# Row sums for the norms: a moving operand of one column where 128 equal ones stood

## The reference, cut to what matters

```python
def layer_norm(x, g, b):            # twice in each of the 4 layers
    mu = jnp.mean(x32, axis=-1, keepdims=True)
    var = jnp.mean(jnp.square(x32 - mu), axis=-1, keepdims=True)
    y = (x32 - mu) * lax.rsqrt(var + LN_EPS) * g + b

def rms_norm_2(x, w):               # three times in the fifth block
    y = x32 * lax.rsqrt(jnp.mean(x32 * x32, axis=-1, keepdims=True) + RMS_EPS) * w
```

## Time and profile before

| | us |
|---|---|
| median of 3 runs | 3677.93 (3677.74 to 3681.67) |
| the profiled execution's own time | 3677.74 |
| its span in the trace | 3675.9 |
| PE busy | 3564.8 (97%) |
| PE weight loads busy | 2998.0 (82%) |
| DVE busy | 1831.4 (50%) |
| ACT, POOL busy | 941.4 (26%), 824.6 (22%) |
| mean granted clock of TensorE | 0.989 |

### The profile page before, as it was taken

How to read it: one execution, slowest core, us unless ns; L and a number is a source line. 1 busy time by engine, 2 the same in 40 slices (tenths; PEclk the granted TensorE clock), 3 DMA queues, 4 the chain that set the end, 5 groups by cost and what they waited for, 6 DMA issues and landing times.

```text
span 3675.9 us, 44420 instructions
## 1 busy us (share of the span) xinstructions
PE 3564.8 (97%) x18618; PEld 2998.0 (82%) x18618; DVE 1831.4 (50%) x2281; ACT 941.4 (26%) x1662; POOL 824.6 (22%) x374
## 2 busy tenths in 40 slices
PE   8989999999999999999999998999999999999998
PEld 6778888898888888688888877888888887788887
DVE  5555334646563346663336555553464445653434
ACT  2552001312230013540103255210141215120102
POOL 2113222311032223122223211322221111222221
PEclk9999999999999999999999999999999999999999
DMA  5312222221122223122222321222212222222222
GB/s 201 104 58 92 101 95 91 93 69 58 64 81 95 101 92 102 62 75 92 103 93 81 109 81 58 95 92 100 84 69 92 81 92 86 98 92 93 103 92 69
DMA packets 57279, 329.58 MB, mean 90 GB/s; under 512 B 5579, under 2 KB 12235, under 8 KB 20348
## 3 DMA queue, kind: packets, MB, share of 16 engines
q1 hardware_dynamic: 44604, 303.79, 23.1%
q10 hardware_dynamic: 12480, 22.96, 1.8%
HBM read 323.96 MB, written 8.80 MB: 91 GB/s over the span
## 4 chain that ended last, share of the span: by engine, by line
PE 87%; DVE 7%; ACT 3%; issue 1%; DMA 1%; POOL 0%; ACTq 0%; DVEq 0%
PE proj L472 23%; PE proj L474 23%; PE proj L473 23%; PE proj L571 2%; PE proj L573 2%; PE proj L572 2%; DVE s L1740 2%; PE proj L505 2%; PE proj L507 1%; PE proj L506 1%; PE mix L738 1%; PE mix L644 1%; PE mix L549 1%; DVE wlo L1634 1%; PE mix L670 1%; DVE h L1774 1%
## 5 line engine op out<-in xcount | busy, mean ns | idle before, releaser
L451 POOL TENSOR_SCALAR whi<-raw 128x2048 fp32r<-128x2048 f32 x286 | 724.3, 2533 | 2575.8 <-DMA raw<-in_stream 2575.8
L472 PE MATMUL proj<-gh,whi 128*128 128x512 f32 x1968 | 785.7, 399 | 14.4 <-DVE wlo L1640 10.5
L474 PE MATMUL proj<-gh,wlo 128*128 128x512 f32 x1968 | 770.9, 392 | 0.0
L473 PE MATMUL proj<-gl,whi 128*128 128x512 f32 x1968 | 770.1, 391 | 0.0
L1634 DVE TENSOR_TENSOR wlo<-raw,whi 128x2048 fp32r<-128x2048 f32 x286 | 702.3, 2458 | 118.7 <-POOL whi L451 108.5
L472 PE MATMUL proj<-xh,whi 128*128 128x512 f32 x1760 | 697.5, 396 | 13.1 <-DVE wlo L1634 5.6
L474 PE MATMUL proj<-xh,wlo 128*128 128x512 f32 x1760 | 691.2, 393 | 0.0
L473 PE MATMUL proj<-xl,whi 128*128 128x512 f32 x1760 | 691.1, 393 | 0.0
L472 PEld LDWEIGHTS proj<-gh,whi 128*128 128x128 f32 x1968 | 370.9, 188 | 108.0 <-issue 15.8
L474 PEld LDWEIGHTS proj<-gh,wlo 128*128 128x128 f32 x1968 | 370.5, 188 | 80.8
L473 PEld LDWEIGHTS proj<-gl,whi 128*128 128x128 f32 x1968 | 371.0, 189 | 78.9 <-issue 2.2
(11 more groups left out here) (295 smaller groups left out, 4338.4 us busy)
## 6 DMA issues: line engine op xcount, KB each, us to landing
raw<-in_stream SPq DMA_DIRECT2D x286, 1024.0 KB, 4.8
da_b<-bias_da ACTq DMA_DIRECT2D x16, 512.0 KB, 3.4
bias_da<-bias_rows ACTq DMA_DIRECT2D x8, 512.0 KB, 9.2
h<-in_x ACTq DMA_DIRECT2D x4, 512.0 KB, 8.7
bias_sw<-bias_table ACTq DMA_DIRECT2D x1, 2048.0 KB, 9.9
pf<-in_p ACTq DMA_DIRECT2D x4, 512.0 KB, 5.6
sw_b<-bias_sw ACTq DMA_DIRECT2D x4, 512.0 KB, 3.5
out_features<-fin SPq DMA_DIRECT2D x8, 256.0 KB, 2.3
```

What stands on the lines that cost most here:

```text
L451: nc.gpsimd.tensor_scalar(whi[SLOT[n]][:, :, :], raw[SLOT[n]][:, :, :], 1.0, 0.0, ALU.mult, ALU.add).then_inc(hi_done, 1)
L472: nc.tensor.matmul(out, wh, ah, start=first, stop=False, skip_group_check=check)
L473: nc.tensor.matmul(out, wh, al, start=False, stop=False, skip_group_check=check)
L474: return nc.tensor.matmul(out, wl, ah, start=False, stop=last, skip_group_check=check)
```

## The change

The matmul of `stats` takes one column of `ones` and writes one column: column 4q + t of the bank, with q = 0 for the sums and 1 for the sums of squares, and t the token tile, 0 to 3. Before it took all 128 columns and wrote 128, at (2q + t % 2) x 128. VectorE reads the two columns of a half next to each other, where it read two columns 128 apart. The number and order of all instructions stay as they were.

```diff
                     for t in range(2 * hf, 2 * hf + 2):
                         for part in range(2):
-                            at = (2 * q + t % 2) * P
-                            last = nc.tensor.matmul(mix[:, 0, at:at + P], total[:, part, t * P:(t + 1) * P], ones[:, :],
+                            last = nc.tensor.matmul(mix[:, 0, 4 * q + t:4 * q + t + 1], total[:, part, t * P:(t + 1) * P], ones[:, 0:1],
                                                     start=part == 0, stop=part == 1, skip_group_check=True)
 ...
                 c = 2 * hf
-                total, squared = mix[:, 0, 0:2 * P:P], mix[:, 0, 2 * P:4 * P:P]
                 dve.wait_ge(M("stats"), 2 * l + hf + 1)
                 if l < 2 * NL:
-                    V.tensor_scalar(m, total, 1.0 / D, None, ALU.mult).then_inc(*own.sig())
+                    V.tensor_scalar(m, mix[:, 0, c:c + 2], 1.0 / D, None, ALU.mult).then_inc(*own.sig())
 ...
-                    V.scalar_tensor_tensor(v, squared, 1.0 / D, v, ALU.mult, ALU.add).then_inc(*own.sig())
+                    V.scalar_tensor_tensor(v, mix[:, 0, 4 + c:6 + c], 1.0 / D, v, ALU.mult, ALU.add).then_inc(*own.sig())
 ...
-                    V.tensor_scalar(v, squared, 1.0 / D, RMS_EPS, ALU.mult, ALU.add).then_inc(*own.sig(M("var_done")))
+                    V.tensor_scalar(v, mix[:, 0, 4 + c:6 + c], 1.0 / D, RMS_EPS, ALU.mult, ALU.add).then_inc(*own.sig(M("var_done")))
```

## The result

The changed kernel takes 3702.06 us (median of 4 runs, 3701.27 to 3708.82) against 3678.99 us for the kernel before (4 runs, 3677.74 to 3681.67): a recorded ratio of 1.0065, with a 95% interval of 1.0048 to 1.0084. It is slower by 23 us. The profiled execution took 3699.42 us, 21.7 more than that of before.

The account below looks back on a forecast made before the run. PE, busy 97% of the span, was taken as the bound; 0 (passes) - 0.1 (ends) + 0 (reads) + 13.5 + 1 (clock) = +14.4 us on 3677.74, so 3692 us. Own range 3684 to 3699, for all 3675 to 3699.

Parts of the forecast that it names:

- The passes: The 304 narrowed matmul passes: weight loads, not columns, pace them at 112 ns, so 0 us.
- rival B: Faster passes: weight loads speed up with fewer columns, 57 ns per pass, 17.3 us gained, 3660.4 us; chance 5%.
- The end of a group: Last pass of each group ends about 106 ns earlier, which counts only in the last border: 0.1 us gained.
- DVE's reads: DVE's 22 reads of two PSUM values, now adjacent: 0 us, with 0.4 us either way.
- The clock: One-column passes leave PE's array quiet around the groups, so more half clock: 13.5 plus 1 us lost; forecast 53%.
- Half 1: Ten of 11 half 1 groups get 3.4 us more at half clock: 10 to 17 us, middle 13.5.
- Half 0: The 11 half 0 groups have no long pause ahead: 1 us lost to the clock, range 0 to 7.
- Rival C: Half 0's groups drop the clock too, half 1's for longer: 17 + 7 = 24 us, 3702; chance 4%.

Follow-up runs that it names:

- e2: One column only in the groups of half 1, against the kernel before: 3689.06 us against 3679.47, ratio 1.0028.
- e1: One column only in the groups of half 0, against the kernel before: 3689.88 us against 3679.47, ratio 1.0031.
- e6: Kernel before plus dummy 128-column matmuls in half 1's waits (9 and 3): 3671.14 us against 3682.13, ratio 0.9969.
- e9: Kernel before plus dummy 128-column matmuls sized to half 1's waits and ahead of two waits for weights: 3665.67 us against 3680.48, ratio 0.9959.
- e4: Changed kernel plus dummy 128-column matmuls in half 1's waits (9 or 3): 3680.68 us against 3679.47 for the kernel before, ratio 1.0004.
- e5: Changed kernel plus the same number of dummy matmuls in half 1's waits, each of one column: 3702.04 us against 3682.13 before, ratio 1.0054.
- e10: One column only in the groups of half 0, run once more for a second trace: 3689.46 us against 3680.48 for the kernel before.

## Why the prediction was wrong in its size

*The passes* (0 us): right. With one column, 17 distances take 1.90 us, 112 ns each. Neither the 26 us by the Trainium skill's floor for short matmuls ("TensorE: Matmul & The Clock Gate", Back-to-back issue gap) nor rival B's 17 us came. Rows with half of the columns were the better guide.

*The end of a group* (-0.1 us): too small to matter either way. The shortest pass is 106 ns shorter, as worked out. In the last border PE waits 0.69 us for the reciprocal as before; from the group's start to `spread` it was 3667.80 - 3665.79 = 2.01 us and is 3689.50 - 3687.76 = 1.74. Of these 0.27 us not all is the shorter pass: before, the clock fell to half at 3666.64, inside the group, and after only at 3689.32.

*DVE's reads* (0 us): nothing seen. There are 38 of them, not 22, since a layer norm reads both sums. Those of L1749 and L1757 (L1747 and L1755 after) took 158 to 160 ns before and 159 to 160 after. The product of span and clock has no room for more than 2 us.

*The clock* (+14.5 us): right in kind, and the mis-sized term. It measured 21.7 us in the profiled executions. By the place where the time at half stands, its two parts came out so:

- Half 1, put at 10 stretches at 1.0 to 1.7 us, middle 13.5. The trace has 64.9 - 34.1 = 30.8 us more at half there, nine stretches, at 1.7 us each 15.4. The sum of stretches was near, but not where they would stand: borders 0 and 8 gained two, border 9 none, and border 6 lost one. The price of 1.0 came from borders in which part of the time at half lay in a wait or ahead of one; an added stretch lies where PE has work nearly throughout, and costs about half of its length. Border 2 shows it, with 2.12 us for one stretch more and some that left the pause.
- Half 0, put at 1 us. The distance from half 0's group to half 1's grew by 1.49, 1.62, 1.18 and 1.48 us in borders 0, 2, 6 and 8, and by at most 0.1 us in the others: 5.8 us. I had called a pause of 1.55 us the nearest row and didn't ask what the group of 16 passes, 1.8 us long, had been doing for the clock as long as it moved 128 columns.

15.4 and 5.8 make 21.2 of the 21.7 us. But the place is not the cause. With only half 1 narrow the kernel costs 9.6 us (e2; 6 to 14 by the interval of its ratio), with only half 0 narrow 10.4 (e1; 7 to 16). By these two, half 1's term of 13.5 is not shown to have been too low, and the step that failed is half 0's: put at 1 us with a bound of 7, because the pauses ahead of its groups are short, and measured at 10.4. Rival C, "the clock falls further", gave 3702 and had 4% of the chance; it is what was measured, though its 17 for half 1 and 7 for half 0 are not how e1 and e2 divide it. The range stopped at 3699 although its own bounds (17 + 7) reached 3702.

The Trainium skill (same page, section What's actually happening) says that the throttle follows how busy the PE has recently been. The traces agree in that the clock stayed up once PE's waits were filled (e6, e9), but being busy in the profile is not enough: over the same passes and loads the mean clock was 1.00 in e4 and 0.83 in e5, with PE busy for 17.09 of 17.49 us and for 19.80 of 20.34.

One thing is not settled. Half 0 alone costs 10.4 us by its median, of which 6 are seen behind half 0's groups in e10's trace. The rest is time at half elsewhere, and in e1's trace it stands behind half 1 groups of 128 columns. Whether it is moved there by the shift in time, which the narrow half 0 groups bring about, or scattered, two traces can't tell. So what one narrow group costs is not shown, only what all 11 of a half cost together. What also wasn't tried is whether fillers could stand in the waits inside the mixers.

## What to carry to other kernels

On an engine that is busy 97% of the time, matmul columns that look wasted can be free, and can even pay: if the weight loads set the pitch, narrowing the moving operand saves nothing, and it can cost clock where TensorE has just waited. Before narrowing, compare two rows with the same weights and different columns; then look at the granted clock behind each wait of TensorE. And multiply span by mean clock in every trace: if two kernels that do the same work give the same product, the clock is the difference, and dummy matmuls in unavoidable waits, no longer than the wait, may win it back (here 14.8 us, 0.4%).

## What the runs showed of the hardware that was not expected

- A matmul pass with one moving column and a full load of weights did not hold the clock when it filled the waits (0.83 over 20.34 us of e5, with PE busy for 19.80 in the profile), while the same pass with 128 columns did (1.00 over the same passes in e4).
- Half of the columns had half of the cost: 64 of 128 cost 11.6 us, one of 128 cost 19 to 23. These are the only two points.
- At a PE busy share of 97% the kernel before still spent 77.6 us at half clock (mean 0.989). PE was idle in 12.8 of them, most of that at the very end; the other 64.8 cost at most half, 32 us.
- One and the same kernel had 61.4 us at half around its half 1 groups in one execution and 34.1 in another (e1, e10; 3697.8 and 3689.5 us).
